# One hybrid decoder layer on one core: the last 512 output columns token tile by token tile, and the shared expert of the first tile between them

## The reference, cut to what matters

```
mix   = merged @ w_out                                # 2048 x 2048
x     = layer_norm(alpha * x + mix, ln1_g, ln1_b)
logits = x @ router_w                                 # 64 experts
idx, w = top-8 of sigmoid(logits) + bias, in 4 of 8 groups
moe   = sum over the 8 experts of w * (silu(x @ w_gate[e]) * (x @ w_up[e])) @ w_down[e]
shared = (silu(x @ ws_gate) * (x @ ws_up)) @ ws_down   # 256 hidden columns
out   = layer_norm(alpha * x + moe + shared, ln2_g, ln2_b)
```

## Time and profile before

| what | us |
|---|---|
| median of 3 runs | 2399.03 |
| lowest and highest of them | 2396.36, 2408.94 |
| the profiled execution's own time | 2413.57 |
| its span, first to last instruction | 2411.7 |

### The profile page before, as it was taken

One profiled execution on the slowest core, in us unless ns is written; L12 is line 12 of the kernel. 1 busy time (PEld: TensorE's weight loads), 2 busy tenths in 40 slices (PEclk: granted clock), 3 DMA queues, 4 the chain that ended last, 5 costly groups with the idle time before them and its releaser, 6 DMA issues.

```text
span 2411.7 us, 34686 instructions
## 1 busy us (share of the span) xinstructions
PE 2267.5 (94%) x14214; PEld 1762.3 (73%) x14214; DVE 1050.6 (44%) x1306; ACT 692.4 (29%) x766; POOL 59.9 (2%) x58
## 2 busy tenths in 40 slices
PE   6999999999999999998989999999999999999985
PEld 5888888888888888887877666666666666666652
DVE  4444559985666666666553122212212222221114
ACT  3334443334344444444330111111111111111110
POOL 0000000000000000001000000000000000000001
PEclk8999999999999999999979999999999999999987
DMA  6565455555455555566553999999999999999970
GB/s 211 181 197 179 141 175 175 176 177 171 140 175 175 182 190 185 174 204 212 182 212 113 421 419 402 395 395 398 405 395 396 396 396 395 395 395 395 399 310 36
DMA packets 250475, 643.35 MB, mean 267 GB/s; under 512 B 5111, under 2 KB 185335, under 8 KB 198060
## 3 DMA queue, kind: packets, MB, share of 16 engines
q1 hardware_dynamic: 249344, 635.46, 69.5%
q0 software_dynamic: 880, 6.32, 0.7%
q10 hardware_dynamic: 188, 0.68, 0.1%
HBM read 640.34 MB, written 2.10 MB: 266 GB/s over the span
## 4 chain that ended last, share of the span: by engine, by line
PE 90%; DVE 4%; issue 3%; ACT 1%; DMA 1%; DVEq 0%; POOL 0%; SPq 0%; PEldq 0%; ACTq 0%; POOLq 0%
PE ps_proj L1292 21%; PE ps_proj L1483 19%; PE ps_proj L1293 10%; PE ps_s L1519 10%; PE ps_t L1538 6%; PE ps_t L1436 5%; PE ps_s L1284 3%; PE ps_proj L1284 3%; PE ps_s L1272 2%; PE ps_t L1272 2%; PE ps_s L1285 1%; PE ps_proj L1285 1%; PE ps_proj L1405 1%; PE ps_s L1273 1%; PE ps_t L1273 1%
## 5 line engine op out<-in xcount | busy, mean ns | idle before, releaser
L1292 PE MATMUL ps_proj<-x_both,w_both 128*128 128x512 f32 x2176 | 772.4, 400 | 21.7 <-DVE w_both L801 11.4
L1293 PE MATMUL ps_proj<-x_both,w_both 128*128 128x256 f32 x2176 | 610.9, 281 | 0.0
L801 DVE TENSOR_TENSOR w_both<-raw,w_both 128x2048 fp32r<-128x2048 f32 x200 | 480.0, 2401 | 216.5 <-ACT w_both L574 216.1
L1292 PEld LDWEIGHTS ps_proj<-x_both,w_both 128*128 128x128 f32 x2176 | 411.4, 189 | 122.5 <-issue 14.4
L1483 PE MATMUL ps_proj<-ring,xt 128*64 128x256 f32 x4224 | 465.1, 381 | 18.7 <-PE ps_s L1519 17.8
L1483 PEld LDWEIGHTS ps_proj<-ring,xt 128*64 128x64 f32 x4224 | 338.3, 137 | 158.9 <-issue 48.2
L1293 PEld LDWEIGHTS ps_proj<-x_both,w_both 128*128 128x128 f32 x2176 | 413.3, 190 | 0.1
L574 ACT ACTIVATE w_both<-raw 128x2048 fp32r<-128x2048 f32 x200 | 380.4, 1907 | 106.3 <-PE ps_proj L1293 37.6
L1519 PE MATMUL ps_s<-ring,ht 128*64 128x512 f32 x1056 | 233.9, 595 | 1.1 <-issue 1.0
L1137 DVE TENSOR_TENSOR y_lo<-ps_s,y_hi 128x1024 fp32r<-128x1024 f32 x66 | 77.7, 1219 | 247.3 <-ACT y_hi L733 247.3
L1129 DVE SCALAR_TENSOR_TENSOR hidden<-ps_proj,slot_w,gate_sig 128x256 f32<-128x256 f32 x33 | 16.0, 484 | 389.0 <-ACT gate_sig L715 360.7
(11 more groups left out here) (258 smaller groups left out, 2112.5 us busy)
## 6 DMA issues: line engine op xcount, KB each, us to landing
raw<-in_w_in_dram SPq DMA_DIRECT2D x80, 2048.0 KB, 8.3
ring<-in_w_gate_dram SPq DMA_DIRECT2D x64, 2048.0 KB, 10.9
ring<-in_w_up_dram SPq DMA_DIRECT2D x64, 2048.0 KB, 14.0
ring<-in_w_down_dram SPq DMA_DIRECT2D x64, 2048.0 KB, 8.8
raw<-in_w_branch_dram SPq DMA_DIRECT2D x12, 2048.0 KB, 8.0
raw<-in_w_out_dram SPq DMA_DIRECT2D x8, 2048.0 KB, 8.2
ring<-in_w_gate_dram SPq DMA_DIRECT2D x4, 1024.0 KB, 11.1
ring<-in_w_up_dram SPq DMA_DIRECT2D x4, 1024.0 KB, 14.4
```

The costliest lines, as they stand in the source:

```text
L801: nc.vector.tensor_tensor(tiles(w_lo, u, w), raw_half(u, w), tiles(w_hi, u, w).bitcast(F32), ALU.subtract).then_inc(s_lo, 1)
L1292: pe.matmul(sums[:, :], hi[:, t, :], x_both[:, :, t, :], start=(t == 0), stop=False)
L1293: ins = pe.matmul(sums[:, 0:TOK], lo[:, t, :], x_hi[:, t, :], start=False, stop=(t == KT - 1))
```

## The change

In the last turn of "out" the four blocks run in the order j = 0, 2, 1, 3: first both halves of tile 0, then both of tile 1. Each block has its own signal and waits for the weights that it needs. The evacuation of the turn before's j = 3 moves behind the split of the last unit. The statistics, the root and the normalizing passes are made for each tile by itself, those of tile 0 ahead of tile 1's last sums.

TensorE then turns tile 0, makes its logits and its shared gate, turns tile 1, makes its logits and its shared gate, and goes on with the counts. The transposes have eight places in six banks in another order and wait for nobody. All four copies of tile 0 are ScalarE's. The shared up products signal tile by tile. ScalarE rounds tile 1's `h_hi` behind the sigmoid, and VectorE takes tile 1's `h_lo` behind the first selection. The job tables move into quad 0, behind its first product, and to another place in SBUF.

```diff
-        job_table = at("job_table", [P, MAX_JOBS, E], F32, 128)
+        job_table = at("job_table", [P, MAX_JOBS, E], F32, 136)
-        tok_bank = y_bank + swing
+        tok_bank = y_bank[2:] + swing + y_bank
...
                         if j >= 3:
+                            if s["name"] == "out" and isinstance(i, int) and i == LAST_OUT:
+                                evacuate(s["name"], i - 1, 3, Unit(s["base"], s["len"], i - 1, 3))
                             evacuate(s["name"], i, j - 3, Unit(s["base"], s["len"], i, j - 3))
+                        elif s["name"] == "out" and isinstance(i, int) and i == LAST_OUT and j == 2:
+                            pass
...
+        LAST_OUT = KT // 4 - 1
+        last_order = (0, 2, 1, 3)
...
+            root(0)                     # ScalarE
+            for n in range(3):
+                take_tokens(n)
+            root(1)
+            take_tokens(3)
+            turn_rows(0)
+            round_rows(0)
+            turn_rows(1)
+            for n in (4, 6):
+                take_tokens(n)
             act.wait_ge(s_logit, 1)
             nc.scalar.activation(scores[:, :, :], swing[0][:, 0:TT * E].rearrange("p (a e) -> p a e", a=TT),
                                  ACT.Sigmoid).then_inc(s_score, 1)
+            round_rows(1)
...
+                    if last and j >= 2:
+                        dve.wait_ge(s_ev[0], units // 2)
+                        if j == 3:
+                            dve.wait_ge(s_ev[1], units // 2)
+                        nc.vector.bn_stats(stats[:, j % 2, i, :], acc[:, j % 2, 512 * i:512 * i + 512]).then_inc(s_stats, 1)
...
+            last_out(2)                 # VectorE
+            normalize(0)
+            last_out(1)
+            last_out(3)
+            normalize(1)
+            leave_rows(0)
+            for n in (5, 7):
...
             weights_of_tokens()
             select_quad(0, False)
+            leave_rows(1)
...
-            count_jobs()
-            job_tables()
...
                 product(2 * q, 0)
-                if not is_first(q):
+                if is_first(q):
+                    count_jobs()
+                    job_tables()
+                else:
...
+            def last_columns(j):        # TensorE
+                r, tt = j // 2 * 2, j % 2
+                hi = w_hi[:, r:r + 2, :].rearrange("p r (t c) -> p r t c", t=KT)
+                both = w_both[:, :, r:r + 2, :].rearrange("p a r (t c) -> p a r t c", t=KT)
+                sums = pair_out(j)
+                pe.wait_ge(s_lo, units - 2 + r)
+                for b in range(2):
+                    pe.wait_ge(s_ev[b], units // 2 - 3 + j // 2)
+                for t in range(KT):
+                    tok = slice(tt * P, (tt + 1) * P)
+                    pe.matmul(sums, merged_hi[:, t, tok], both[:, :, :, t, :], start=(t == 0), stop=False)
+                    ins = pe.matmul(sums[:, 0:2 * P], merged_lo[:, t, tok], hi[:, :, t, :], start=False, stop=(t == KT - 1))
+                ins.then_inc(s_mm, 1)
...
+            for j in last_order:
+                last_columns(j)
+            turn_tokens(0)
+            pe.wait_ge(s_tokact, 4)
+            pe.wait_ge(s_rw, 16)
+            logits(0)
+            pe.wait_ge(s_w[0], 16)
+            for r in range(2):
+                pe.wait_ge(s_ev[r], units // 2)
+            shared_in(0, 0)
+            turn_tokens(1)
+            pe.wait_ge(s_tokact, 6)
+            pe.wait_ge(s_tokdve, 2)
+            logits(1).then_inc(s_logit, 1)
+            shared_in(0, 1).then_inc(s_unit, 1)
...
-            shared_in(1)
+            pe.wait_ge(s_w[1], 16)
+            shared_in(1, 0).then_inc(s_shgu, 1)
+            shared_in(1, 1).then_inc(s_unit, 1)
```

More of the change, by code:

```diff
@@ L317, in wide_out, with stream @@
             return [ps_s[1], ps_t][u.bank][:, :].rearrange("p (h a c) -> p h a c", h=2, a=2)
-        def stream(eng, per_unit, evacuate, after, before_last):
+        def stream(eng, per_unit, evacuate, after):
             prev = None
@@ L342, in stream @@
                         body(i)
+                elif s["name"] == "out":
+                    with eng.Fori(1, s["n"] - 1) as i:
+                        body(i)
+                    body(s["n"] - 1)
                 else:
@@ L681, in after, with root, turn_rows, take_tokens @@
                                              ACT.Copy).then_inc(s_mhi, 1)
-            stream(act, split, evacuate, after, lambda: None)
+            stream(act, split, evacuate, after)
             act.dma_start(rw[:, :, :], router_w[0].rearrange("(p t) e -> p t e", p=P)).then_inc(s_rw, 16)
-            act.wait_ge(s_var, 1)
-            nc.scalar.activation(std, var_eps, ACT.Sqrt).then_inc(s_std, 1)
-            for n in range(0, 8, 2):
+            def root(tt):
+                act.wait_ge(s_var, tt + 1)
+                nc.scalar.activation(std[:, tt:tt + 1], var_eps[:, tt:tt + 1], ACT.Sqrt).then_inc(s_std, 1)
+            def turn_rows(tt):
+                act.wait_ge(s_shifted[tt], 1)
+                nc.scalar.activation(h_turn[:, tt, :].rearrange("p (t q) -> p t q", t=KT),
+                                     acc[:, tt, :].rearrange("p (q t) -> p t q", t=KT), ACT.Copy).then_inc(s_hturn, 1)
+            def take_tokens(n):
                 act.wait_ge(s_tokturn, n + 1)
@@ L804, in evacuate @@
             def evacuate(name, i, j, u):
-                dve.wait_ge(s_mm, u.n + 1)
+                last = name == "out" and isinstance(i, int) and i == LAST_OUT
+                dve.wait_ge(s_mm, u.n - j + last_order.index(j) + 1 if last else u.n + 1)
                 ps = ps_proj[u.bank]
@@ L866, in evacuate @@
                 elif name == "out":
-                    if j == 0 and isinstance(i, int):
+                    if isinstance(i, int) and i == 0 and j == 0:
                         dve.wait_ge(s_xr, 16)
@@ L1009, in batch, with normalize @@
                 dve.wait_ge(s_dve, dve_done(k))
[L1012 to L1019, removed]
+            stream(dve, split, evacuate, after)
+            def normalize(tt):
+                dve.wait_ge(s_stats, 7 + tt)
+                step(nc.vector.bn_aggr(mean_var[:, tt, :], stats[:, tt, :, :]))
+                nc.vector.tensor_scalar(var_eps[:, tt:tt + 1], mean_var[:, tt, 1:2], LN_EPS, None,
+                                        ALU.add).then_inc(s_var, 1)
+                dve.wait_ge(s_std, tt + 1)
+                step(nc.vector.reciprocal(rstd[:, tt:tt + 1], std[:, tt:tt + 1]))
+                dve.wait_ge(s_lnp, 32)
                 step(nc.vector.scalar_tensor_tensor(out=acc[:, tt, :], in0=acc[:, tt, :], scalar=mean_var[:, tt, 0:1],
@@ L1023, in _, with last_out, leave_rows @@
                                                in1=ln_b[:, :], op0=ALU.mult, op1=ALU.add).then_inc(s_shifted[tt], 1)
[L1025 to L1029, removed]
-            for tt in range(TT):
+            def last_out(j):
+                evacuate("out", LAST_OUT, j, Unit(BASE_OUT, 4, LAST_OUT, j))
+            def leave_rows(tt):
                 dve.wait_ge(s_hhi, tt + 1)
@@ L1375, in _, with turn_tokens, logits @@
                 if not s["unroll"]:
[L1376 removed]
+                    with pe.Fori(1, s["n"] - (name == "out")) as i:
                         for j in range(s["len"]):
                             multiply(name, i, j, Unit(s["base"], s["len"], i, j))
[L1380 to L1393 removed]
+            def last_columns(j):
[11 more added lines that the diff above has]
+                ins.then_inc(s_mm, 1)
+            def turn_tokens(tt):
+                pe.wait_ge(s_shifted[tt], 1)
+                rows = acc[:, tt, :].rearrange("p (q t) -> p t q", t=KT)
+                for n in range(4 * tt, 4 * tt + 4):
+                    t = n % 4 * 4
+                    for k in range(4):
+                        ins = pe.transpose(tok_bank[n][:, k * P:(k + 1) * P], rows[:, t + k, :], ident[:, :])
+                    ins.then_inc(s_tokturn, 1)
+            def logits(tt):
                 for t in range(KT):
```

54 lines of the change are left out of this document (16 added, 38 removed).

## The result

The changed kernel takes 2391.11 us (median of 21 runs, 2377.73 to 2397.42) against 2404.42 us (21 runs, 2386.30 to 2415.56) of the kernel before on the same chips: a ratio of 0.9951, 95% interval 0.9929 to 0.9972, or some 12 us less by the ratio (the medians lie 13.3 us apart). The forecast was 2380.4 us, 18.6 us under the kernel before. The direction was right and the median lies inside the range, but by the ratio the gain is 6 to 7 us smaller than forecast.

What follows compares the result with a forecast made beforehand. TensorE was taken to bound the expert loop, which starts behind a serial stretch of idle, then slow TensorE. -20.1 + 2.1 - 0.55 = -18.6 us from the median 2399.03 gave 2380.4 us, range 2375 to 2391.5.

Steps and rivals of the forecast that it cites:

- part 3: From the columns' end to the gather, TensorE's new order at full clock takes 42.7 us, gaining 20.1 us.
- 8.9 of idleness, some 11 of half clock: The two pieces of the 20.1 us gain: TensorE's wait for the norm, and its slow work up to the gather.
- the stretch belongs to every execution, so I take the same 18.6 from the median: Applied the gain priced on the profiled execution (2413.57 us) to the median of three runs, 2399.03 us.
- the gap ahead of block 2: In the last column turn, TensorE waits 2.1 us for VectorE's evacuation, behind two weight splits.
- the waits for the tokens: TensorE waits between each tile's transposes and logits: 1.4 us for tile 0, 0.85 us for tile 1.
- from the columns' end to the gather: Transposes, waits, logits and gates of both tiles, counts and shared up: together 42.7 us, before 62.8.
- The job tables are worth: Moving the tables into quad 0 starts the first expert pair 0.55 us earlier and delays nothing.
- the case of a loop paced by its weights: Expert loop limited by the weight stream, so the change gains nothing at the end: 2399 us, chance 0.04.
- Full clock throughout: TensorE's clock never falls in the changed stretch: 2380.4 us, own range 2377 to 2384, chance 0.54.
- one fall: Clock drops once, in a light stretch or the 2.1 us wait: up to 5.4 us back, 2385.8 us, chance 0.25.
- Two falls: Clock drops in both light stretches of transposes, wait and logits: 10.8 us back, 2391.2 us, chance 0.14.
- the rule of the Trainium skill: Transposes don't count as busy for the clock like products; by it both light stretches run down, 2391.2 us, chance 0.14.

Runs made afterwards that it cites:

- e5: The kernel before, unedited, traced a second time: 2400.96 us, one execution.
- e6: The kernel before, unedited, traced a third time: 2400.16 us, one execution.
- e10: The kernel before, unedited, a fourth trace: 2388.18 us, one execution.
- e11: The kernel before, unedited, a fifth trace: 2401.88 us, one execution.
- e1: The changed kernel, unedited, timed once more against the kernel before: 2388.49 us against 2397.99, ratio 0.9953.
- e13: The changed kernel, unedited, traced again: 2393.51 us, one execution.
- e14: The changed kernel, unedited, traced again: 2379.15 us, one execution.
- e15: The changed kernel, unedited, traced again: 2390.83 us, one execution.
- e7: The kernel before with only its job tables moved behind the first product of quad 0: 2399.23 us, one execution.
- e16: The kernel before with 36 unread products in its wait for the norm, a third look: 2406.66 us, one execution.
- e8: The kernel before with 36 unread products in its wait for the norm, timed: 2406.63 us against 2399.04, ratio 1.0021.
- e9: The changed kernel, last-turn blocks waiting for their own bank only, plus 26 unread products ahead of the output projection: 2383.93 us against the kernel before's 2399.73, ratio 0.9936.
- e3: The changed kernel with each block of the last turn waiting for its own bank alone: 2388.84 us, one execution.
- e4: The changed kernel with both norms behind the last sums, as before, keeping its new TensorE order: 2409.86 us, one execution.

## Why the gain was smaller than forecast

**All executions together.** The stage, in every trace of the two unedited kernels (those of before are the earlier trace rows's, e5, e6, e10 and e11; those of after the first, e1, e13, e14 and e15):

| kernel | stage, us | mean |
|---|---|---|
| before | 110.9, 109.2, 100.6, 100.6, 100.6 | 104.4 |
| after | 91.6, 91.6, 93.5, 91.9, 95.3 | 92.8 |

The means differ by 11.6 us, which is what the two timed comparisons measured (0.9951 and 0.9953, 11 to 12 us). Five traces of a kind are few, but every timed execution has its mean granted clock listed, and these agree. The kernel before has a mean of 0.9785 and a span of 2398.3 us over 61 executions, the changed one 0.9816 and 2387.0 us over 33. With c the mean clock, 2 x (1 - c) x span is the time at the lower level, since each microsecond there counts half: 103 us and 88 us. The change removes 15 us of half clock on average (give or take 2, one standard error), where the clock records of the profiled pair show 37 (117 and 80 us). In the five and five traces the half clock in and just ahead of the stage is on average 17 and 2 us, again 15 less.

**The step that failed** is in the forecast's part 3, "8.9 of idleness, some 11 of half clock", together with the sentence of the sum that "the stretch belongs to every execution, so I take the same 18.6 from the median". The idleness does belong to every execution (8.97 or 8.98 us in each further trace). The half clock doesn't. Taking the stages whose logits ran at full clock, 100.6 and 91.6, the gain without any cost of half clock is 9.0 us. What comes on top for the half clock is 10.3 us in the pair forecast from (110.9 - 100.6, of which 0.4 is a slower pace of the column products, told in the last section), but on average only 104.4 - 100.6 = 3.8 us, less the 92.8 - 91.6 = 1.2 us that the changed kernel itself loses. The term was worth 2.6 us, not 10 to 11. Other executions entered the forecast only on the other side, in its range, as ones whose clock comes back later; none of the further four is longer. The warning was in the forecast's own table: the three runs of before had their median 14.5 us under the profiled execution. That execution was unusually long, and part of its length was exactly the term being priced.

**The steps that held**, in the first trace after: the gap ahead of block 2 is 1.93 us, forecast 2.1; the norm of tile 0 is hidden; the waits for the tokens are 1.18 and 0.88 us against 1.4 and 0.85; logits of one tile take 3.6 to 3.8 us against 3.55, a gate 7.0 against 6.95; from the columns' end to the gather it is 1267.91 - 1225.4 = 42.5 us against 42.7. The counts follow tile 1's gate directly. The job tables are worth 0.6 us (e7) against 0.55 and delay nothing. No wait on a transfer appeared, and the expert loop kept its length (first pair to the end: 2411.7 - 1318.4 = 1093.3 us before, 2384.5 - 1292.7 = 1091.8 after), so the case of a loop paced by its weights is out. The length of the loop doesn't depend on when it begins: it is 1090.7 to 1094.7 us in all eighteen traces.

**The clock after the change.** Full clock throughout had 0.54, one fall 0.25, and of five unedited executions three were of the first kind and two of the second, at 1.9 and 3.6 us of cost and not the 5.4 allowed for. Two falls were not seen in these five. On the rule of the Trainium skill (TensorE: Matmul & The Clock Gate, Part 4) that transposes don't count as busy the way products do: in e6, e10 and e11 the level came back during the transposes, with only transposes and waits since 8.98 us of idleness, so as a strict rule it doesn't hold for these float32 transposes. That falls come shortly behind transposes and a wait, in the logits (e5, e15, e16), may be in its spirit, but no run separates the transposes from the logits as their cause, and in most executions they don't come.

**What stays open.** Why the level comes back and falls at different points of identical work wasn't settled; only that it does. The kernel before with fillers (e8) timed slower than without them, by 0.2%, and no trace of it shows where. That e9's filler and bank edit give the 2 us that the traces suggest (at least 1.4 for the filler, 0.5 in e3's stage for the bank) or more (the median is 5 to 7 us lower, the mean span 2383.6 against 2387.0) can't be told from the spread. Of the 16 further traces each shows one execution, so the split into 3.8 and 1.2 us rests on five each, and could well be off by 2 to 3 us, one standard error of the difference.

## What to carry to other kernels

An idle time like this one may be credited in full, since every traced execution had it. A half-clock stretch behind it may not: trace several executions, compare the profiled one with the median of the runs, and credit the average (here 4 us of an apparent 10, and less what the new order loses itself). The remedy that paid was to let work fill the pause, not to fill it with unread products: fillers helped in the one place where dense work followed directly (e9), and not where another wait and light work came next (e8, e16).

## What the runs showed of the hardware

The level came back at different points behind the same pause. Sixteen transposes of tile 0 behind 8.98 us of idleness took 3.4 to 3.7 us in all five traces, but the 64 logits behind them 7.3, 11.3 or 13.7 us.

The level also fell while TensorE was busy without a gap. In six of the eighteen traces (e4, e5, e7, e9, e15, e16) logits began at a granted clock of 1.00, and 2.2 to 2.7 us into them it went to 0.50 and stayed there for 6.8 or 13.7 us. In e6, e10 and e11 the same 64 logits ran at 1.00 from end to end. In all six, transposes and a wait of 0.8 to 1.2 us stood ahead of the logits, but so they did where no fall came.

The pair of a 512-column and a 256-column product has two paces at the same granted clock, and a stretch keeps one of them until TensorE is next held up. Groups of TensorE between 780 and 1090 us, the kernel before as first profiled and then e5 (busy us, mean ns of one):

```profile
L1292 PE MATMUL ps_proj<-x_both,w_both 128*128 128x512 f32 x593 | 209.8, 399 | 0.0
```

```profile
L1292 PE MATMUL ps_proj<-x_both,w_both 128*128 128x512 f32 x612 | 212.4, 391 | 0.0
```

The same products last 399 or 391 ns, and successive pairs start 353 or 347 ns apart. The stretch that they are part of took 361.4 us in 11 of the 18 traces and 354.6 in the other seven, of both kernels alike, with nothing in between. It lies ahead of everything that was changed. What decides between the two paces isn't shown. It makes a good part of the spread of single executions: e13, which has the slower pace there and between 40 and 240 us, trails e14, which has the faster one in both, by 4.3 us at the start of that stretch, 11.2 us at its end, 13.8 us at the first expert pair and 14.3 us at the end. A difference of 12 us needs many runs to be seen.
